# Dilated-window layer: query, key and value projections of six units as 2x2 block products with seven products

## The reference

```python
kv = (rmsnorm(x, g_kv) @ w_kv).reshape(b, t, N_DIL, 2, N_KV_B, HEAD_DIM)     # 3 dilations, 4 kv heads
k  = rope(rmsnorm(kv[:, :, :, 0], k_norm), pos)
q  = rope(rmsnorm((rmsnorm(x, g_attn) @ w_q).reshape(b, t, N_DIL, N_HEADS_B, HEAD_DIM), q_norm), pos)
# per dilation g (windows 128/1, 512/4, 2048/16): local attention; outputs combined by softmax of their lse; then @ w_o
```

## Time and profile before

| | us |
|---|---|
| median of 3 runs | 1362.58 (1358.84 to 1363.71) |
| the profiled execution | 1356.8 |
| its span, first to last instruction | 1355.0 |
| PE / DVE / POOL / ACT busy in the span | 1268.2 / 639.5 / 494.6 / 331.5 |
| DMA, mean rate | 246 GB/s |

### The profile page before, as it was taken

How to read it: one execution, slowest core, us unless ns; L and a number is a source line. 1 busy time by engine, 2 the same in 40 slices (tenths; PEclk the granted TensorE clock), 3 DMA queues, 4 the chain that set the end, 5 groups by cost and what they waited for, 6 DMA issues and landing times. The chain is left out here.

```text
span 1355.0 us, 20817 instructions
## 1 busy us (share of the span) xinstructions
PE 1268.2 (94%) x8580; PEld 890.1 (66%) x8580; DVE 639.5 (47%) x1018; ACT 331.5 (24%) x667; POOL 494.6 (37%) x417
## 2 busy tenths in 40 slices
PE   8999999999999977899999999999998999998786
PEld 6788887446566644458877877877846666664453
DVE  3587775614522211173558558558436472221114
ACT  2223332302122212140115005005005312221122
POOL 4456644101111111006876576576450111111101
PEclk9999999999999999999999999999999999999998
DMA  8446636577699999961113013013050899999997
GB/s 317 136 158 222 217 110 217 182 310 289 267 416 417 419 418 420 411 250 58 53 56 98 9 56 98 9 56 97 9 141 3 330 364 418 418 419 419 419 420 288
DMA packets 92768, 318.82 MB, mean 235 GB/s; under 512 B 32969, under 2 KB 45401, under 8 KB 66564
## 3 DMA queue, kind: packets, MB, share of 16 engines
q1 hardware_dynamic: 77956, 279.95, 53.1%
q0 software_dynamic: 13536, 33.29, 6.8%
q10 hardware_dynamic: 1184, 4.26, 0.8%
HBM read 300.19 MB, written 33.28 MB: 246 GB/s over the span
## 5 line engine op out<-in xcount | busy, mean ns | idle before, releaser
L2063 PE MATMUL ps<-slots 128*128 128x384 f32 x768 | 262.0, 495 | 0.7 <-DVE vo L2362 0.3
L2063 PEld LDWEIGHTS ps<-slots 128*128 128x128 f32 x768 | 203.4, 270 | 43.0 <-issue 3.2
L1214 PE MATMUL ps<-slots,oT 128*64 128x256 f32 x1344 | 176.4, 387 | 31.6 <-DMA slots<-in_w_up 26.8
L1214 PEld LDWEIGHTS ps<-slots,oT 128*64 128x64 f32 x1344 | 120.0, 139 | 81.9 <-issue 29.9
L1726 POOL DMA_INDIRECT y_rows<-ysb,idx x30 | 30.1, 1005 | 360.0 <-DVE ysb L1249 349.5
L1240 DVE TENSOR_TENSOR sg<-sg,ps 64x256 f32<-64x256 f32 x64 | 26.4, 413 | 244.7 <-ACT sg L1237 244.7
L1237 ACT ACTIVATE sg<-ps 64x256 f32<-64x256 f32 x64 | 24.4, 380 | 238.9 <-PE ps L1214 238.9
L1249 DVE COPY ysb<-ps 64x512 f32<-64x512 f32 x60 | 41.6, 693 | 85.8 <-PE ps L1232 85.8
L2300 ACT ACTIVATE slots<-slots,neg 128x128 f32<-128x128 f32 (+1 forms) x192 | 64.1, 417 | 54.8 <-DVE neg L2407 49.3
L602 PE MATMUL ps<-xnT_a,wA 128*128 128x260 f32 (+1 forms) x320 | 75.3, 391 | 1.5 <-DVE xnT_a L866 1.4
L2571 POOL TENSOR_TENSOR late_b<-tok 128x1600 f32<-128x1600 f32 x12 | 36.3, 3024 | 99.1 <-DVE tok L2370 99.1
(11 more groups left out here) (328 smaller groups left out, 2262.5 us busy)
## 6 DMA issues: line engine op xcount, KB each, us to landing
slots<-in_w_gate SPq DMA_DIRECT2D x42, 1024.0 KB, 26.5
slots<-in_w_up SPq DMA_DIRECT2D x42, 1024.0 KB, 28.3
slots<-in_w_down SPq DMA_DIRECT2D x36, 1024.0 KB, 28.8
slots<-in_unit_weights_b SPq DMA_DIRECT2D x12, 1536.0 KB, 6.8
wA<-in_qkv_pairs_a SPq DMA_DIRECT2D x24, 512.0 KB, 3.6
apart<-in_w_down SPq DMA_DIRECT2D x8, 1024.0 KB, 28.9
spare<-in_w_down SPq DMA_DIRECT2D x8, 1024.0 KB, 26.2
apart<-in_w_up SPq DMA_DIRECT2D x6, 1024.0 KB, 28.9
```

The source lines that it names most:

```text
L1214: last = nc.tensor.matmul(bank(q)[lo:lo + CAP, 0:FE], x[:, k, :], wt[:, k, :], start=(k == 0), stop=(k == KT - 1))
L2063: last = nc.tensor.matmul(bank(i % 2)[:, 0:UW], xT[:, kt, cols], wB[:, g, kt, :], start=(kt == 0), stop=(kt == KT - 1))
```

## The change

Six units, the second and third dilation of head groups 1 to 3 (n = 4, 5, 7, 8, 10, 11), are computed as a 2x2 block product: tokens in halves (residues 0 and 1, residues 2 and 3) by rows in halves, weights by rows and columns in halves (192 columns), with seven half-size products in place of eight. The sums and differences of tokens (`mix_x`, four tiles in `apart`, contiguous) are made once on DVE, in head group 0. Those of weights (`t1` to `t4`) are made per unit by five DVE instructions: three of 768 columns, two of 384. Products are read by eight parts: PARTS maps chunks 0, 1, 2 to two parts each, chunk 3 to one, chunk 4 to the samples. Since sums of tokens must be of normed tokens, DVE multiplies `xT` in place by the factor, residue by residue (`normalize`), while unit 1 is projected; the factors come as a row on all partitions (`rsb`) by one more DMA, and evictions from unit 2 on no longer scale. On DVE `scale(j+1, 0)` moves behind two groups of evictions, and `scale(j+1, 1)` moves: for j = 0 ahead of `ahead(1, 0)`, for j = 1 and 2 ahead of `ahead(0, 4)`.

```diff
+            PARTS = ((0, 1), (2, 3), (4, 5), (6,), (7,))
+            def mixed(n):
+                return n > NDIL and n % NDIL > 0
...
                     sp.dma_start(rsr[:, :], rs_rows.rearrange("(i r) -> i r", r=4)).then_inc(s_rsi, 16)
+                    sp.dma_start(rsb, rs_rows.partition_broadcast(128)).then_inc(s_rsi, 16)
...
+                    def mixed_part(n, part):
+                        g, i, w = n % NDIL, chunk0[n] + part, wB[:, n % NDIL]
+                        upper, lower = x_res[:, 0:HK], x_res[:, HK:KT]
+                        if part == 0:
+                            pe.wait_ge(s_ws, scaled0[n] + 2)
+                            pe.wait_ge(s_mix, 8)
+                        elif part in (1, 3, 5):
+                            pe.wait_ge(s_ws, scaled0[n] + (4, 5, 7)[part // 2])
+                        pe.wait_ge(s_ev, i - 1)
...
+                            tokens = (upper[:, :, 0:2], mix_x[1], lower[:, :, 0:2], mix_x[2], mix_x[0], lower[:, :, 2:4], mix_x[3])[part]
+                            for c in range(2):
+                                for k in range(HK):
+                                    cols = (w[:, k, 0:UH], t2[:, k], w[:, HK + k, 0:UH], t3[:, k], t1[:, k],
+                                            t4[k // 2][:, k % 2], w[:, HK + k, UH:UW])[part]
+                                    last = nc.tensor.matmul(bank(i % 2)[:, UH * c:UH * c + UH], tokens[:, k, c, :], cols, ...)
...
+                    def room(j, g):
+                            if n == 1:
+                                dve.wait_ge(s_rsi, 32)
...
+                    def evict_mixed(j, g, part):
+                        if part == 0:
+                            V.tensor_copy(first_p, got).then_inc(s_ev, 1)
+                        elif part in (1, 3):
+                            V.tensor_tensor(early if part == 1 else late, first_p, got, ALU.add).then_inc(s_ev, 1)
+                        elif part == 2:
+                            V.tensor_copy(tok[:, g, 0:2, HD:UH], got[:, :, HD:])
+                            V.tensor_copy(vo[:, j % 2, g, 0:2, :], got[:, :, 0:HD]).then_inc(s_ev, 1)
...
+                    def normalize(c):
+                        dve.wait_ge(s_proj, chunk0[1] + c + 1)
+                        dve.wait_ge(s_rsi, 32)
+                        rows = xT[:, :, c:SEQ:4]
+                        V.tensor_tensor(rows, rows, rsb[:, c:SEQ:4].unsqueeze(1).to_broadcast([128, KT, 128]), ALU.mult).then_inc(s_mix, 1)
+                    def mix_tokens(step):
+                        x11, x12, x21, x22 = [x_res[:, HK * i:HK * i + HK, c:c + 2] for c in (0, 2) for i in range(2)]
...
+                        V.tensor_tensor(mix_x[out], one, other, op).then_inc(s_mix, 1)
+                    def mix_weights(j, g, steps=range(5)):
+                        for step in steps:
...
+                            dve.wait_ge(s_ws, scaled0[n] + (2, 3, 2, 4, 4)[step])
+                            V.tensor_tensor(out, one, other, ALU.subtract).then_inc(s_ws, 1)
...
+                        if j:
+                            mix_weights(j, 2, (0, 1, 2))
+                            evict_mixed(j, 2, 0)
+                            mix_weights(j, 2, (3, 4))
+                            evict_mixed(j, 2, 1)
+                        else:
+                            ahead(0, 0)
+                        ahead(0, 1)
                         if more:
                             scale(j + 1, 0)
-                        ahead(0, 0)
-                        ahead(0, 1)
...
                         soft(j, 0, 2)
+                        own(2)
+                        if j and more:
+                            scale(j + 1, 1)
                         ahead(0, 4)
                         soft(j, 0, 3, s_m0)
+                        own(3)
+                        if not j:
+                            scale(j + 1, 1)
                         ahead(1, 0)
+                        if more:
+                            mix_weights(j + 1, 1, (0, 1))
                         ahead(1, 1)
                         soft(j, 1, 0)
+                        if more:
+                            mix_weights(j + 1, 1, (2,))
                         ahead(1, 2)
                         soft(j, 1, 1)
+                        if more:
+                            mix_weights(j + 1, 1, (3, 4))
                         ahead(1, 3)
-                        if more:
-                            scale(j + 1, 1)
                         ahead(1, 4)
```

More of the change, by code:

```diff
@@ L2067, in project @@
                                 pe.wait_ge(s_xc, NT)
[L2068 to L2071 removed]
+                            last = sample_rows(i, g)
+                        last.then_inc(s_proj, 1)
@@ L2190, in _ @@
                     project(0, 0, 4)
-                    for c in range(NCHUNK):
+                    for c in range(NT):
                         project(0, 1, c)
@@ L2346, in evict @@
                         n = 3 * j + g
-                        i = NCHUNK * n + c
+                        if mixed(n):
+                            for part in PARTS[c]:
+                                evict_mixed(j, g, part)
+                            return
+                        i = chunk0[n] + c
                         dve.wait_ge(s_proj, i + 1)
@@ new lines, in mix_weights @@
+                    def mix_weights(j, g, steps=range(5)):
+                        n, w = 3 * j + g, wB[:, g]
+                        b11, b12, b21, b22 = [w[:, HK * i:HK * i + HK, UH * h:UH * h + UH] for i in range(2) for h in range(2)]
+                        for step in steps:
+                            if step == 0 and j + g > 2:
+                                dve.wait_ge(s_proj, chunk0[n - 3 + g] + 6)
+                            out, one, other = ((t1, b12, b11), (t2, b22, t1), (t3, b22, b12), (t4[0], b21[:, 0:HK // 2], t2[:, 0:HK // 2]),
+                                               (t4[1], b21[:, HK // 2:], t2[:, HK // 2:]))[step]
+                            dve.wait_ge(s_ws, scaled0[n] + (2, 3, 2, 4, 4)[step])
+                            V.tensor_tensor(out, one, other, ALU.subtract).then_inc(s_ws, 1)
```

115 lines of the change are left out of this document (88 added, 27 removed).

## The result

The changed kernel takes 1396.77 us by median (1395.85 to 1404.71, four runs) against 1362.95 us for the kernel before on the same chip (1358.84 to 1363.71, four runs): a ratio of 1.0283, 95% interval 1.0259 to 1.0307, about 34 us slower. The profiled execution spans 1395.3 us, 40.3 more than the one of before, which lay 6 us under its kernel's median while the changed kernel's lay at its own. The forecast was 1392.6 us in a range of 1372 to 1408.

What follows compares the result with a forecast made beforehand. PE, in its queue's order, was taken to bound the dilated layer, level with POOL before the third keys' turn. Terms 15.0 + 14.6 + 1.3 - 0.9 = +30.0 us on the median 1362.58 gave 1392.6 us, range 1372 to 1408.

Steps and rivals of the forecast that it cites:

- PE's work: Six mixed units: step-4 loads set 0.213 us an interval, so a unit takes 20.6 us against 20.7, no gain.
- The start: Layer start and head group 0: evictions, token multiplications, mixes and scalings delay the third keys' turn by 15.0 us, to 710.9.
- The "+1.3" for the broadcast: Layer start: unit 1's evictions wait for the 256 KB broadcast of factors, landing at 630.2, 1.3 us later.
- The lock: DVE and POOL, both reading two SBUF tiles, exclude each other, except during POOL's power of 4.36 us.
- the sign: POOL's norm and rope spans for the third unit of head groups 0 to 2 at 26 to 31 us.
- Head groups 1 and 2: Longer second groups (3.95 us) and POOL's later end (3.3 us) before the third keys' turn: +7.3 us each.
- Head group 3: No scaling and no next unit there: +3.95 less 2.6 for one short group, +1.3 us.
- The weighing stretches: Score-weighing stretches after the third keys' turn: some 0.3 us gained for each of three units, -0.9 in all.
- "loads hidden": Rival: PE's step-4 loads hide, units lose 2.4 us of PE each, lock as forecast: +18, 1380.6 us; chance 0.15.
- "order alone": Rival: step-4 loads at 0.213 us, no exclusion between DVE and POOL: +8.4, 1371.0 us; chance 0.12.
- "faster": Rival: loads hide at 0.162 us, and POOL and DVE meet rarely: -6.7, 1355.9 us; chance 0.07.
- The rival of DVE at half speed: Rival: DVE at half speed on steps of 16 bytes, eight token instructions at +1.2 each: +40, 1402.6 us; chance 0.20.

Runs made afterwards that it cites:

- e_contig_mix1: Changed kernel with parts 0, 2 and 5 reading contiguous mixed tokens and the five weight subtractions cut to one column: layer 26.95 us shorter.
- e_norm1: Changed kernel with the four token multiplications by the norm cut to one column of one block: 1395.44 us, ratio 1.0278.
- a_order: Changed kernel with DVE's two-tile work (mixes, weight scaling) moved out of POOL's third norm and rope, nothing left out: 1374.30 us, ratio 1.0131.
- e_rsb: Changed kernel with the factors' broadcast on its own semaphore, so unit 1's evictions wait only for the small transfer: ratio 1.0277.
- e_order_undo: Changed kernel with the next group's second weight scaling, in head groups 1 and 2, back behind the fourth softmax step: ratio 1.0277.
- e_mix1: Changed kernel with the five weight subtractions of a mixed unit cut to one column: layer 6.3 us shorter.
- e_busy4: Changed kernel with four idle products of 512 columns where PE waits for POOL before the third unit's turn: 1396.48 us, ratio 1.0263.
- b_order: Kernel before, with only the next group's second weight scaling moved ahead of the samples' eviction in head groups 1 and 2: 1368.40 us, ratio 1.0082.

## Why the prediction was right, point by point

The direction and the causes at the start and in the head groups were right. That the total came within 4.2 us is in part luck: one term had the wrong sign and was 8.9 us off, others were too large, and the traces differ by 36.4 us in the layer where the medians differ by 33.8.

**PE's work: mechanism right, size low.** "PE's gain from seven products in place of eight is then nothing": shown, by the two paces and by e_contig_mix1, in which contiguous trains, once the mixes are out of the way too, give the time back. The interval taken for step 4, 0.213 us from two loads in a row, was 0.237; a unit is 21.7, not 20.6. Contiguous loads last 190 ns and hide under 0.162, loads at step 4 last 330 and set 0.237. The Trainium skill (TensorE: Matmul & The Clock Gate, LDWEIGHTS) prices a load by its columns alone, 107 ns for 128; at step 4 the trace disagrees (0.237 us). The Trainium skill (SBUF — State Buffer, Specifications (TRN2)) says that memory lines are 16 bytes and that each access to a new line costs; at step 4 every fp32 value is in a line of its own, and both the loads and DVE's multiplications of tokens (2.0 us) agree with it.

**The start: right in kind, its exact number by luck.** Forecast +15.0 for the turn of the third keys, to 710.9; measured 710.92. The layer began 0.95 earlier, so its start grew by 15.9. The steps were off in size: multiplications 2.0, not 1.2; POOL's first front until 652.6, not 650.8, the second until 680.8, not 677.8, the third from 681.6, not 680.3; against that the third front took 29.3, not 30.6. e_norm1 and a_order divide it: 5.25 us for the multiplications, 7.1 for what meets the third front and delays its start; the other 3.6 no run takes away. The "+1.3" for the broadcast isn't a term of its own: the first eviction did come 2.7 later after POOL's first norm began, but e_rsb gives that back and the turn doesn't move.

**The lock: shown.** POOL's norm and rope stretch by what DVE does beside it (e_order_undo) and their third front is back at 23.2 when DVE keeps away (a_order, and e_mix1 in head groups 1 and 2). It was 29.3, 25.0 and 25.0 in the changed kernel, where 26 to 31 was named as the sign, so the sign was met in head group 0 only.

**Head groups 1 and 2: +7.3 forecast, +6.1 and +5.7 measured.** Samples' eviction: 795.10 + 1.28 = 796.4, which is 11.1 after the second scores end at 785.3 (forecast 11.3). The second scores end 3.8 us later than before (forecast 3.95, though its own terms, three times 0.85 and 1.1, make 3.65). POOL's third front was 25.0 us rather than 25.9, and PE's stall on part 1's eviction 0.20 rather than 1.1: at 0.237 PE comes later by about as much. Head group 3: +0.7, forecast +1.3.

**The weighing stretches: the step that failed.** The sum had "some 0.3 us for each of the three units in the score-weighing stretch" as a gain. They grew by 2.3, 3.3 and 2.4 us, 8.0 in all where -0.9 stood. The forecast named the stands at the turn (5 to 7 us; measured 3.9, 5.1 and 5.1) but priced only the stand itself. e_busy4 puts 1.6 to 2.6 of each on the clock that falls after it; the other 0.7 no run divides further.

Together: 15.9 + 6.1 + 5.7 + 0.7 + 8.0 = 36.4 us of the layer against 30.0 forecast; by medians it is 33.8. The rivals: "loads hidden" fell by the step-4 intervals, "order alone" by POOL's fronts and e_order_undo, "faster" with both (its own terms make -6.9, not -6.7). The rival of DVE at half speed had its condition nearly met: the eight token instructions, each taken as 1.2 in the forecast and 2.4 in the rival, took 2.00 to 2.47 us, and one that waited 4.11. Its +40 for the whole wasn't reached; why the extra time stayed under cover wasn't traced. So the forecast was nearer in its total than in this price, and that is luck too.

## What to carry to other kernels

Fewer products pay only if each is still bound by its moving columns: here 192 columns (0.162 us) no longer cover a load at a step of 16 bytes (0.237), where 384 (0.323) did. Ask of every new DVE instruction with two SBUF inputs what GpSimd runs at that moment, and put it where GpSimd idles, or beside its power, which left DVE alone here; one reordering was worth 1.5% here. Then ask whether DVE has room where the work goes: W0 grew by 2.1 us. And when one cost is taken away and nothing moves, take away two: paths of the same length hide each other (3.9 and 6.3 us alone, 27 together).

## What the runs showed of the hardware that was not expected

**A stand can cost twice.** Waits of 2.3 to 5.1 us of PE were followed by slower matmuls, at a granted clock that fell to the lower of its two levels, 1.2 in place of 2.4 GHz (0.50 in the rows right behind the stand of 5.12): twelve turning matmuls in 2.8 us in place of 1.53, the samples' part in 2.75 in place of 1.51, a train of sixteen in 4.48 in place of 2.77. In b_order a stand of 3.38 us cost 1.3 more behind it; in the changed kernel 1.6 to 2.6. Filled with four idle products (3.60 us) it costs nothing behind it. It doesn't follow every stand: in a_order PE stood 3.73 us ahead of the samples' part at the layer's start, and that part took 1.51, while a stand of 2.33 in W0 was followed by a train of 4.90 in place of 3.95. What decides it no run here shows. PE's timeline of a_order at the two places:

```profile
643.26 1.51 PE L2103 MATMUL ps<-slots 128*8 128x96 f32 x64 [3.73 <-DVE vo L2421]
...
708.02 4.90 PE L2127 MATMUL ps<-slots 128*128 128x192 f32 x16 [2.33 <-DVE slots L2400]
```

The Trainium skill (TensorE: Matmul & The Clock Gate, What's actually happening) says that TensorE's clock falls to half when it idles; the rows at the turns agree (0.50 behind 5.12 us), those at the layer's start show a stand without it.

**DVE at a step of 16 bytes.** A product of two SBUF tiles with 1024 columns takes 2.00 us at step 4, also when POOL runs its power, which elsewhere doesn't disturb DVE; a difference of 768 contiguous columns takes 0.95 (a_order).
